# One plan for a block's mixers: chunk ends among the levels, tiles taken out a row later, masks in the exponent

## The chip, the cores and the metric

The kernel runs on one core of a Trainium2 chip. The metric is the device time of one execution in microseconds. The engines are TensorE (PE; PEld for its weight loads), VectorE (DVE), ScalarE (ACT), GpSimd (POOL) and SyncE (SP), which issues most DMAs. Each works through its own queue in program order; semaphores tie the queues together.

## The reference

Two transformer blocks are computed in sequence over 512 tokens of 1024 columns, all in float32. The change touches the mixers of the first block only:

```
proj = einsum('bsd,de->bse', h, w_in)               # 26.5 units of 256 columns, 25 of them in the changed part
o_a = diff attention: softmax(q1 k1) - lam * softmax(q2 k2), times v, 4 heads, 4 query blocks of 128
o_b = hgrn2: gated recurrence S_t = diag(a_t) S_(t-1) + k_t v_t^T, o_t = S_t^T q_t, forward + backward, 4 heads
o_c = gla:   the same recurrence, forward + backward, 4 heads (two at a time here)
merged = g_a * (o_a @ w_up_a) + g_b * (o_b @ w_up_b) + g_c * (o_c @ w_up_c)
x = x + gt_m * (merged @ w_out)
```

The vector `mod` (shift, gain, gate of each part) is `silu(c) @ ada_w + ada_b`; two thirds of it are needed only behind the mixers. The MLP of the first block and the whole second block (windowed attention, a spatial gating unit, two gated FFNs) follow.

## The kernel before

A dense product is made of units: 8 x 128 rows of a weight by 256 columns, 1 MB, loaded by SP into RAW (two buffers, 8 KB a partition), split in four parts into a high half WH (ACT, `split`) and a low half WL (POOL), and multiplied in three passes (HHI x WH, HLO x WH, HHI x WL). A unit gives two tiles of 128 x 512 in PSUM, each of 24 matmuls; a "natural" unit (cv, bv, av) has the tokens on the partitions and 96 matmuls of 256 columns. Each tile is taken out of PSUM (`evict`) by ACT or DVE.

A recurrence r (0 and 1 for gla, two heads each; 2 to 5 for hgrn2, one head each) treats chunks of 128 tokens in seven levels of halves (lv 0 to 6) and one of single tokens (lv 7). A level is `differ` (DVE: Am less a reference column, into DD), `expo` (ACT: exp of each half, in place), `scale` (DVE: KL = k x DD over all columns, then QL for the lower and the upper half, each with a 0/1 vector that switches off one direction), `product` (PE: 4 matmuls of 128 x 128 in float32 for a head) and `collect` (DVE, under a mask, into SCT). DD, QL and KL have two buffers each, by level; the product has PSUM banks 4 and 5 in turns. After the last level come the chunk ends, one after the other: `ends`, `reach` (POOL), `turn` (PE), `state` (PE), `carry` (DVE), `read` (PE). `lag` makes Am out of the cumulated decay with two DVE instructions.

Attention takes a head and a block of 128 queries in four steps: logits for both maps (PE), bias, maximum and scaled maximum (DVE), exponent (ACT), weights (DVE), transposes (PE) and a copy to WT (ACT). The values follow once a head, in one product of 512 columns (`attend_v`), then the head's norm.

The order is set by generators of steps, each step a list of operations that every engine's program walks through alike, skipping what is not its own. `merged` mixes streams by weights. The first merge (from 124 us) mixes `gla` with `projections` (units bz, bq, bv, bg, av, aq, ak and the decays); units cv and cg and the low-rank gate stand ahead of it. The second (from 336 us) mixes `hgrn`, `attention` and `gates`: 12 gate units, whose tiles go through T0 to DRAM (`spill`), and the 16 later units of `ada_w`, which DVE multiplies by eight instructions of 256 columns each. A tile is taken out in the step right behind its last matmul. Behind the second merge the units `up` read all of o_a, o_b, o_c and the spilled gates.

```
    def first_merge(self):
        return merged((self.gla(), WA[0]), (self.projections(), WA[1]))
    def second_merge(self):
        return merged((self.hgrn(), WB[0]), (self.attention(), WB[1]), (self.gates(), WB[2]))
```

Of the kernel before, what the change touches and what calls it, by code (L numbers as in the profile page):

```python
# [7 lines left out]
ACT = mybir.ActivationFunctionType  # L8
# [3 lines left out]
T = 512  # L12
EPS = 1e-6
LAM_INIT = 0.2
KB = 1024
# [5 lines left out]
WA = (77, 110)  # L21
WB = (142, 72, 130)


# [33 lines left out]
def unit_order():  # L58
# [10 lines left out]
    cols("w_in", "cv", full, [(3072, 256)])  # L69
    cols("w_in", "cg", full, [(3328, 256)])  # L70
    for p in range(2):
        c = []
        for h in (2 * p, 2 * p + 1):
            c += [(1792 + 64 * h, 64), (2048 + 64 * h, 64)]
        cols("w_in", "bz", full, c)
    cols("w_in", "bq", full, [(1536, 256)])
    cols("w_in", "bv", full, [(2304, 256)])
    cols("w_in", "bg", full, [(2560, 256)])
    for i in range(2):
        cols("w_in", "av", full, [(1024 + 256 * i, 256)])  # L80
    for i in range(2):
        cols("w_in", "aq", full, [(256 * i, 256)])
        cols("w_in", "ak", full, [(512 + 256 * i, 256)])
    a = 8
    for j in range(4):
        for g in range(3):
            cols("w_in", "gate", full, [(3616 + 1024 * g + 256 * j, 256)])
            for _ in range(2 if g == 0 else 1):
                cols("ada_w", "ada", full, [(256 * a, 256)])
                a += 1  # L90
# [115 lines left out]

def merged(*streams):

    live = [[iter(s), n, 0] for s, n in streams]
    out = []  # L210
    while live:
        x = min(live, key=lambda q: q[2] / q[1])
        step = next(x[0], None)
        if step is None:
            live.remove(x)
        else:
            out += step
            x[2] += 1
    return out


class Plan:


    def __init__(self):
# [16 lines left out]
        self.first = self.first_merge()  # L242
        self.second = self.second_merge()
# [29 lines left out]
    def place(self):  # L273

        at, four, six, seven = self.at, [0, 1, 2, 3], list(range(6)), list(range(7))
        for tag, n, m in (("cqk", 0, 2), ("lr", 0, 1), ("cv", 0, 2), ("cg", 0, 2), ("bz", 0, 2), ("bz", 1, 2), ("bq", 0, 2), ("bv", 0, 2),
                          ("bg", 0, 2), ("av", 0, 2), ("av", 1, 2), ("aq", 0, 2), ("ak", 0, 2), ("aq", 1, 2), ("ak", 1, 2)):
            self.take(four, *[(at[tag, n], j) for j in range(m)])
        self.take([3], *[(at["gate", n], m) for n in range(12) for m in range(2)])
# [40 lines left out]
    def rows(self, tag, n):  # L320

        i = self.at[tag, n]
        nx = self.after(i)
        part = {(0, 2): 0, (0, 4): 1, (0, 6): 2, (1, 0): 3}
        for m in range(2):
            for k in (0, 2, 4, 6):
                yield [("gemm", i, m, k)] + ([("split", nx, part[m, k])] if (m, k) in part else [])
            yield [("evict", i, tag, n, m)]

    def rows_nat(self, tag, n):  # L330
        i = self.at[tag, n]
        nx = self.after(i)
        for g in range(2):
            for h in range(2):
                yield [("nat", i, g, h)] + ([("split", nx, 2 * h), ("split", nx, 2 * h + 1)] if g == 0 else [])
            yield [("evict", i, tag, n, g)]

    def projections(self):
        for p in range(2):
            yield from self.rows("bz", p)  # L340
            yield []
        for p in range(2):
            yield from (self.rows_nat("bv", 0) if p else self.rows("bq", 0))
            yield []
            for n in range(7):
                yield [("decay", p, n)]
        yield from self.rows("bg", 0)
        yield []
        for i in range(2):
            yield from self.rows_nat("av", i)  # L350
            yield []
        for i in range(2):
            for tag in ("aq", "ak"):
                yield from self.rows(tag, i)
                yield []

    def recur(self, r):
        yield [("lag", r)]
        yield [("differ", r, 0)]
        yield [("expo", r, 0), ("differ", r, 1)]  # L360
        yield [("scale", r, 0), ("expo", r, 1)]
        for lv in range(8):
            yield [("product", r, lv)]
            yield [("scale", r, lv + 1)] * (lv < 6) + [("differ", r, lv + 2)] * (lv < 5)
            yield [("collect", r, lv)] + [("expo", r, lv + 2)] * (lv < 5)
        yield [("ends", r)]
        yield [("reach", r)]
        yield [("turn", r)]
        yield [("state", r)]
        yield [("carry", r)]  # L370
        yield [("read", r)]

    def gla(self):
        for n in range(3):
            yield [("gate_c", n)]
        for P in range(2):
            yield from self.recur(P)
            for n in range(3):
                yield [("norm", "c", P, n)]

    def hgrn(self):
        for u in range(2):
            for h in range(2):
                yield from self.recur(2 + 2 * u + h)
            for n in range(3):
                yield [("norm", "b", u, n)]

    def attention(self):
        for h in range(4):
            for qb in range(4):  # L390
                for n in range(4):
                    yield [("attn", h, qb, n)]
            yield [("attn_v", h)]
            for n in range(3):
                yield [("norm", "a", h, n)]

    def gates(self):
        a, left = 8, []
        for j in range(4):
            for g in range(3):  # L400
                n = 3 * j + g
                i = self.at["gate", n]
                nx = self.after(i)
                rows = [[("gemm", i, m, k)] if k < 8 else [("evict", i, "gate", n, m)] for m in range(2) for k in (0, 2, 4, 6, 8)]
                yield left + rows[0]
                yield rows[1]
                at = 2
                for _ in range(2 if g == 0 else 1):
                    for s in range(3):
                        yield [("ada", a, s)] + rows[at]  # L410
                        at += 1
                    a += 1
                part = 0
                for row in rows[at:]:
                    if row[0][0] == "gemm":
                        row = row + [("split", nx, part)]
                        part += 1
                    yield row
                left = [("split", nx, p) for p in range(part, 4)]
        yield left  # L420

    def first_merge(self):
        return merged((self.gla(), WA[0]), (self.projections(), WA[1]))

    def second_merge(self):
        return merged((self.hgrn(), WB[0]), (self.attention(), WB[1]), (self.gates(), WB[2]))


def build(nc, wts, xt, vec, mixc, masks, distw, wst, bsr, out, spill):
# [57 lines left out]
    KBt = place("KBt", q0 + 36 * KB, [4, T])  # L487
    GB = place("GB", q0 + 44 * KB, [2, T])
    QB = place("QB", q0 + 48 * KB, [4, T])
# [11 lines left out]
    DD = [place(f"DD{i}", f + 2 * KB * i, [T]) for i in range(2)]; f += 4 * KB  # L501
    QL = [place(f"QL{i}", f + 2 * KB * i, [T]) for i in range(2)]; f += 4 * KB
    KL = [place(f"KL{i}", f + 2 * KB * i, [T]) for i in range(2)]; f += 4 * KB
# [7 lines left out]
    SB = [place(f"SB{i}", q0 + 64 * KB + 2 * KB * i, [T]) for i in range(2)]  # L511
    WT = place("WT", q0 + 68 * KB, [4, T])
# [28 lines left out]

    sgn = {"c": ("sgnc", "fc", "bc", 1.0 / 16.0), "b": ("sgnh", "fh", "bh", 1.0)}

    def scan(r):

        if r < 2:
            return (QKC[:, r, 0, :], QKC[:, r, 1, :], PC[:, r, :], [(0, 64, 128 * r, 0), (64, 64, 128 * r + 64, 64)], VC, "c",
                    ("qc", 0), ("qc", 1), ("decay_c", r), ("vc", 1))
        h = r - 2
        return (QB[:, h, :], KBt[:, h, :], ZB[:, h, :], [(0, 128, 64 * h, 64 * (h % 2))], VB, "b",  # L550
                ("qb", h // 2), ("kb", h), ("decay_b", h), ("vb", 1))

# [5 lines left out]
    def branch(kind, n):  # L558
        if kind == "a":
            return 0, 2, 128, ones, SC[:, 3:4], None, (OA[:, n, 0, :], OA[:, n, 1, :]), T0[1][:, :], SS[:, :]  # L560
# [45 lines left out]

    FOLD = (0, 3, 6)
    FOLD = (0, 3, 6)
# [3 lines left out]
    def sync_program(q):  # L612
# [20 lines left out]
        for step in P.first + P.second:  # L633
# [9 lines left out]
            if step[0] == "split" and step[2] == 3 or step[0] == "ada" and step[2] == 1:  # L643
                i = step[1] if step[0] == "split" else U["ada", step[1]]
                while done < min(i + 2, len(units) - 1):
                    done += 1
                    load(done)
# [35 lines left out]
    def tensor_program(q):  # L683
# [208 lines left out]
        tiles_nat(U["cv", 0], hk("mix"))  # L892
# [1811 lines left out]
```

## Time and profile before

| what | value |
| --- | --- |
| median of 3 runs | 2562.35 us (2560.0 to 2563.56) |
| the profiled execution's own time | 2563.16 us |
| its span, first to last instruction | 2561.3 us |
| mean granted TensorE clock | 0.962 of full speed |
| PE, DVE, ACT, POOL busy | 92%, 48%, 38%, 41% of the span |
| instructions | 30127 |

The profile's own execution is 0.8 us above the median. Busy shares are of the whole span. PEclk is the clock that TensorE was granted, in parts of full speed; matmuls are pipelined and their ends are modelled, so PE may read as busy while it runs at the lower clock. In a row of groups the idle time and what ended it stand behind the bar.

### The profile page before, as it was taken

The page shows a single profiled execution, that of the slowest core. Times are in us where ns is not written, and L with a number is a line of the kernel's source. Part 1 is how long each engine was busy: PE and PEld are TensorE (multiplying, and loading weights), DVE is VectorE, ACT ScalarE, POOL GpSimd, SP SyncE. Part 2 cuts the span into 40 slices and gives each one's busy share as a digit, 9 for nine tenths or more (in the row PEclk, how much of TensorE's full clock was granted, in tenths as well). Part 3 has the DMA queues.
Part 4 walks back from the last instruction along what each step waited for, and adds up shares of the span by engine and source line. Part 5 has one row for each costly group of instructions (what it writes and reads, how often), then busy time and mean ns, then how long its engine had stood idle before and what let it go on. Part 6 is the DMA issues. An engine that isn't in the chain of part 4 may idle for free. (4 is left out here: it accounts for less than half of the span.)

```text
span 2561.3 us, 30127 instructions
## 1 busy us (share of the span) xinstructions
PE 2346.7 (92%) x12110; PEld 1962.7 (77%) x12110; DVE 1228.5 (48%) x1968; ACT 965.8 (38%) x1801; POOL 1046.0 (41%) x806
## 2 busy tenths in 40 slices
PE   5868987887799999999889999999999999999997
PEld 4656865665488888887678888888988888888887
DVE  4165376788455222146557624445143444743354
ACT  2345233344445233244436322235332224522233
POOL 2333322223154444453134444445444444454443
PEclk9877998889899999999999999999999999999999
DMA  5321133332342222232011222222222222232221
GB/s 214 105 66 50 50 111 103 119 120 100 115 172 83 99 99 83 98 109 71 28 50 67 99 99 98 100 83 99 86 80 99 82 95 72 81 116 84 102 94 66
DMA packets 42508, 239.87 MB, mean 94 GB/s; under 512 B 4992, under 2 KB 7040, under 8 KB 17152
## 3 DMA queue, kind: packets, MB, share of 16 engines
q1 hardware_dynamic: 39312, 231.23, 25.5%
q10 hardware_dynamic: 3056, 6.70, 0.9%
q8 instruction: 96, 1.57, 0.2%
q14 instruction: 44, 0.36, 0.0%
HBM read 226.38 MB, written 8.39 MB: 92 GB/s over the span
## 5 line engine op out<-in xcount | busy, mean ns | idle before, releaser
L2427 POOL TENSOR_TENSOR WL<-RAW,WH 128x512 fp32r<-128x512 f32 (+1 forms) x724 | 949.8, 1342 | 1220.9 <-ACT WH L1212 1209.2
L695 PE MATMUL PS<-HHI,WH 128*128 128x512 f32 (+1 forms) x1688 | 667.0, 395 | 31.4 <-DVE HLO L1759 8.9
L695 PE MATMUL PS<-HHI,WL 128*128 128x512 f32 (+1 forms) x1688 | 646.7, 383 | 0.0
L695 PE MATMUL PS<-HLO,WH 128*128 128x512 f32 (+1 forms) x1688 | 646.4, 383 | 0.0
L1212 ACT ACTIVATE WH<-RAW 128x512 fp32r<-128x512 f32 (+1 forms) x724 | 395.9, 612 | 386.1 <-PE PS L695 362.0
L695 PEld LDWEIGHTS PS<-HHI,WH 128*128 128x128 f32 x1688 | 324.2, 192 | 114.9 <-issue 23.5
L695 PEld LDWEIGHTS PS<-HHI,WL 128*128 128x128 f32 x1688 | 323.7, 192 | 61.8
L695 PEld LDWEIGHTS PS<-HLO,WH 128*128 128x128 f32 x1688 | 324.9, 192 | 57.2 <-issue 1.9
L695 PE MATMUL PS<-UF,WH 128*128 128x512 f32 (+1 forms) x832 | 223.9, 357 | 0.0
L1753 DVE TENSOR_TENSOR T<-PS,R 128x512 f32<-128x512 f32 x112 | 76.9, 689 | 215.4 <-PE PS L695 204.8
L695 PEld LDWEIGHTS PS<-UF,WH 128*128 128x128 f32 x832 | 148.3, 189 | 22.7
L695 PE MATMUL PS<-WH,HHI 128*128 128x256 f32 x544 | 160.1, 294 | 4.4 <-DVE HLO L1759 2.4
L695 PE MATMUL PS<-UP,WH 128*128 128x512 f32 x512 | 157.7, 389 | 0.0
L695 PE MATMUL PS<-WH,HLO 128*128 128x256 f32 x544 | 156.8, 288 | 0.0
L695 PE MATMUL PS<-WL,HHI 128*128 128x256 f32 x544 | 156.6, 288 | 0.0
L1753 DVE TENSOR_TENSOR Y<-PS,Y 128x512 f32<-128x512 f32 x96 | 66.1, 690 | 176.3 <-PE PS L695 176.3
L695 PE MATMUL PS<-UF,WL 128*128 128x512 f32 (+1 forms) x416 | 148.3, 356 | 0.0
L695 PEld LDWEIGHTS PS<-WH,HHI 128*128 128x128 f32 x544 | 107.2, 197 | 10.1 <-POOL WL L2427 3.8
L695 PEld LDWEIGHTS PS<-UP,WH 128*128 128x128 f32 x512 | 96.1, 188 | 20.0
L695 PEld LDWEIGHTS PS<-WH,HLO 128*128 128x128 f32 x544 | 107.5, 198 | 0.3 <-issue 0.2
L695 PEld LDWEIGHTS PS<-WL,HHI 128*128 128x128 f32 x544 | 107.2, 197 | 0.0
L1695 ACT ACTIVATE TG<-TG 128x512 f32<-128x512 f32 x44 | 27.8, 632 | 207.0 <-DVE TG L1759 207.0
(328 smaller groups left out, 3329.4 us busy)
## 6 DMA issues: line engine op xcount, KB each, us to landing
RAW<-in_wts SPq DMA_DIRECT2D x192, 1024.0 KB, 4.8
spill<-T SPq DMA_DIRECT2D x24, 256.0 KB, 5.5
RAW<-in_wts SPq DMA_DIRECT2D x8, 768.0 KB, 4.3
GT<-spill SPq DMA_DIRECT2D x20, 256.0 KB, 5.0
FW<-in_wts SPq DMA_DIRECT2D x4, 1024.0 KB, 15.5
X<-in_xt SPq DMA_DIRECT2D x1, 2048.0 KB, 16.7
out_x<-X SPq DMA_DIRECT2D x16, 128.0 KB, 1.7
X<-in_xt SPq DMA_DIRECT2D x2, 768.0 KB, 9.9
```

The costliest lines, as they stand in the source:

```text
L695: return e.matmul(o_, l, r, start=start, stop=stop)
L1212: e.activation(WH[s][:, cs], RAW[i % 2][:, cs], ACT.Copy).then_inc(*up("w_hi", ("w_hi", i, p)))
L1695: e.activation(G, G, ACT.Gelu_apprx_tanh).then_inc(*up("a_ev", ("gelu", name, j)))
L1753: return e.tensor_tensor(o_, a, b, f)
L2427: return e.tensor_tensor(o_, a, b, f)
```

## The change

- Both merges become one row of steps. `placed` gives each stream a first row and a gap: the 25 dense units have 8 rows each (a row is two k-slices of a tile, 6 matmuls); all recurrences run in one stream from row 9, a step every 1.1 rows; attention from row 75, a step every 1.7; the decays of hgrn2 from rows 19 and 30. cv and cg join the row.
- The levels of all six recurrences form one sequence, so that the first levels of r + 1 are prepared beside the last of r; the chunk ends of r stand among its own levels 1 to 5, `read` and the norm in those of r + 1.
- A tile is taken out at the second row of the tile behind it.
- The 0/1 vector moves into the exponent, as a bias of 0 or -1e30. DD is 2 x 512 wide: `expo` has two more ACT instructions, with that bias, for the q part; `scale` is one DVE instruction of 1024 columns over q and k, which stand side by side (QKC, QKB). QL and KL are gone.
- `lag` is two ACT copies for hgrn2 and four for gla.
- The product has one bank for hgrn2 (4). Dense tiles have four banks up to unit 8, then 3 and 5.
- Attention's values are made by blocks of 128 queries, one block later; WT holds one block. WT and SB no longer share memory with GT.
- The 16 later ada units are cut as 4 row blocks by 512 columns and stand one in each of the dense units 8 to 23: DVE works 8 instructions of 512 columns for a pair of them, and PE folds a pair at once.

```diff
-WA = (77, 110)
-WB = (142, 72, 130)
+DENSE = [("cv", 0), ("bz", 0), ("bz", 1), ("cg", 0), ("bq", 0), ("bv", 0), ("av", 0), ("aq", 0), ("ak", 0), ("av", 1), ("aq", 1), ("ak", 1),
+         ("bg", 0)] + [("gate", n) for n in range(12)]
+GATE_C, DECAY, RECUR, ATTEND = (1, 2), ((19, 1.5), (30, 1.5)), (9, 1.1), (75, 1.7)
...
+def placed(*streams):
+    at = [(start + gap * i, s, i, step) for s, (steps, (start, gap)) in enumerate(streams) for i, step in enumerate(steps)]
+    return [x for *_, step in sorted(at, key=lambda p: p[:3]) for x in step]
...
+            for m in range(2):
+                for row in range(4):
+                    r = 4 * m + row
+                    step = [("nat", i, m, row // 2)] * (row % 2 == 0) if natural else [("gemm", i, m, 2 * row)]
+                    yield step + beside[r] + (late if row == 1 else [])
+                late = [("evict", i, tag, n, m)]
...
+        for r in range(6):
+            for k in range(8):
+                g = 7 * r + k
+                one, two, three = [("product", r, k)], [], [("collect", r, k)]
+                if k < 7 and g + 1 < len(LEVELS):
+                    two.append(("scale", *LEVELS[g + 1]))
+                if k < 7 and g + 2 < len(LEVELS):
+                    two.append(("differ", *LEVELS[g + 2]))
+                    three.append(("expo", *LEVELS[g + 2]))
...
         def expo(r, lv):
-            e.activation(D[:, :, 0:m], D[:, :, 0:m], ACT.Exp, scale=-s).then_inc(*up("a_mix", ("expo_lo", r, lv)))
-            e.activation(D[:, :, m:2 * m], D[:, :, m:2 * m], ACT.Exp, scale=s).then_inc(*up("a_mix", ("expo", r, lv)))
+            e.activation(Q[:, :, 0:m], K[:, :, 0:m], ACT.Exp, scale=-s, bias=SC[:, b[0]:b[0] + 1])
+            e.activation(Q[:, :, m:2 * m], K[:, :, m:2 * m], ACT.Exp, scale=s, bias=SC[:, b[1]:b[1] + 1]).then_inc(*up("a_mix", ("expo_q", r, lv)))
+            q.wait_ge(*at(("expo_q", r, lv)))
+            e.activation(K[:, :, 0:m], K[:, :, 0:m], ACT.Exp, scale=-s)
+            e.activation(K[:, :, m:2 * m], K[:, :, m:2 * m], ACT.Exp, scale=s).then_inc(*up("a_mix", ("expo", r, lv)))
...
         def scale(r, lv):
-            tt(Ko, Ki, D, MUL)
-            stt(Qo[:, :, 0:m], Qi[:, :, 0:m], v(bs), D[:, :, 0:m], MUL, MUL)
-            stt(Qo[:, :, m:2 * m], Qi[:, :, m:2 * m], v(fs), D[:, :, m:2 * m], MUL, MUL).then_inc(*up("d_mix", ("scaled", r, lv)))
+            D = level(r, lv)[:, :, :]
+            tt(D, both, D, MUL).then_inc(*up("d_mix", ("scaled", r, lv)))
...
+    def product_bank(r, n):
+        return 4 + (n if r < 2 else 0)
```

Two places of the queues show it. On DVE, in an hgrn2 recurrence beside attention; KL, QL, DD and SCT are the recurrence's, SB and SC attention's, SQ and MOD the ada units'. Before, two levels:

```order
L1753 TENSOR_TENSOR KL_106<-KBt,DD_102 128x512
L1759 SCALAR_TENSOR_TENSOR QL_104<-QB,V,DD_102 128x32x8 x2
L1753 TENSOR_TENSOR DD_101<-Am,ZB 128x512
L2083 RECIPROCAL SC<-SC 128x2
L1756 TENSOR_SCALAR SB_116<-SB_116,SC 128x512
L1759 SCALAR_TENSOR_TENSOR SB_115<-SB_115,SC,SB_116 128x512
L2017 COPY_PREDICATED SCT_107<-MASK,PS 128x512
L1753 TENSOR_TENSOR KL_105<-KBt,DD_101 128x512
L1759 SCALAR_TENSOR_TENSOR QL_103<-QB,V,DD_101 128x64x4 x2
L1753 TENSOR_TENSOR DD_102<-Am,ZB 128x512
```

After, two levels:

```order
L1765 TENSOR_TENSOR DD_101<-QKB,DD_101 128x1024
L1765 TENSOR_TENSOR DD_100<-Am,ZB 128x512
L1765 TENSOR_TENSOR MOD<-PS,V 128x4
L2015 COPY_PREDICATED SCT_102<-MASK,PS 128x512
L1768 TENSOR_SCALAR SQ<-RAW_64,CC 128x512
L1771 SCALAR_TENSOR_TENSOR SQ<-RAW_64,CC,SQ 128x512
L1765 TENSOR_TENSOR DD_100<-QKB,DD_100 128x1024
L1765 TENSOR_TENSOR DD_101<-Am,ZB 128x512
```

Three instructions of a level's scaling have become one; the ada work comes in pairs of 512 columns.

On ACT, in the same part of the program; WH is a split, T a gate tile taken out, SB the two exponents of an attention block, WT its weights. Before:

```order
L1438 ACTIVATE DD_102<-DD_102 128x32x8
L1533 ACTIVATE T_74<-PS 128x512
L1497 ACTIVATE SB_115,SC<-SB_115,SC 128x512
L1497 ACTIVATE SB_116,SC<-SB_116,SC 128x512
L1212 ACTIVATE WH_66<-RAW_63 128x512
L1437 ACTIVATE DD_101<-DD_101 128x64x4
L1438 ACTIVATE DD_101<-DD_101 128x64x4
```

After:

```order
L1508 ACTIVATE SB_110,SC<-SB_110,SC 128x512
L1508 ACTIVATE SB_111,SC<-SB_111,SC 128x512
L1441 ACTIVATE DD_101<-DD_101,SC 128x32x8
L1442 ACTIVATE DD_101<-DD_101,SC 128x32x8
L1444 ACTIVATE DD_101<-DD_101 128x32x8
L1445 ACTIVATE DD_101<-DD_101 128x32x8
L1541 ACTIVATE T_74<-PS 128x512
L1514 ACTIVATE WT<-PS 128x512
```

A level has four exponents instead of two, and they still stand behind attention's two.

## Rows read from the trace of the kernel before

**Rows 1.** The page: busy time, and the span in 40 slices.
```profile
PE 2346.7 (92%) x12110; PEld 1962.7 (77%) x12110; DVE 1228.5 (48%) x1968; ACT 965.8 (38%) x1801; POOL 1046.0 (41%) x806
...
PE   5868987887799999999889999999999999999997
PEclk9877998889899999999999999999999999999999
```

**Rows 2.** Busy time of each engine by stretch, whose columns the second line names.
```profile
core 0: us, PE busy (x) PEld busy (x) DVE busy (x) ACT busy (x) POOL busy (x), PEclk, DMA share, GB/s
92.00:124.00 32.00, 32.00 (x175) 28.34 (x175) 3.85 (x15) 9.71 (x16) 12.16 (x11) 0.91 0.27 99
124.00:336.00 212.00, 176.82 (x1012) 144.78 (x1010) 110.58 (x176) 97.19 (x149) 78.80 (x54) 0.87 0.17 58
336.00:650.00 314.00, 251.33 (x1116) 187.10 (x1115) 246.36 (x461) 118.75 (x251) 83.39 (x59) 0.89 0.33 112
650.00:692.00 42.00, 23.06 (x83) 13.75 (x83) 13.88 (x36) 22.13 (x39) 8.87 (x8) 0.80 0.12 39
```

**Rows 3.** The same view, of a stretch inside the first merge and one behind it.
```profile
250.00:325.00 75.00, 75.00 (x481) 62.50 (x480) 28.57 (x57) 22.76 (x45) 24.00 (x19) 1.00 0.20 71
875.00:900.00 25.00, 25.00 (x112) 20.71 (x111) 4.27 (x6) 7.81 (x15) 11.51 (x10) 1.00 0.24 85
```

**Rows 4.** Groups of instructions, 80 to 692 us: a level of a recurrence.
```profile
L1753 DVE TENSOR_TENSOR KL<-KBt,DD 128x512 f32<-128x512 f32 x28 | 25.7, 918 | 0.3 <-ACT DD L1438 0.2
L1759 DVE SCALAR_TENSOR_TENSOR QL<-QB,V,DD 128x256 f32<-128x256 f32 x56 | 36.7, 696 | 0.0
L1753 DVE TENSOR_TENSOR DD<-Am,ZB 128x512 f32<-128x512 f32 x28 | 23.3, 833 | 0.0
L1437 ACT ACTIVATE DD<-DD 128x256 f32<-128x256 f32 x42 | 17.6, 419 | 72.2 <-DVE DD L1753 72.0
L2017 DVE COPY_PREDICATED SCT<-MASK,PS 128x512 f32<-128x512 uint8 x56 | 39.2, 727 | 17.5 <-PE PS L695 17.5
L1753 DVE TENSOR_TENSOR ZB<-ZB,G 128x1024 f32<-128x1024 f32 x4 | 4.9, 1220 | 1.2 <-ACT G L1431 1.1
```

**Rows 5.** One line's instructions, least, median and longest ns, 336 to 689 us.
```profile
L1759 DVE SCALAR_TENSOR_TENSOR SQ<-RAW,CC,SQ x112: 466/485/1502, 340.2 to 637.7; 128x256 f32<-128x256 f32 x112
L1759 DVE SCALAR_TENSOR_TENSOR QL<-QB,V,DD x56: 471/478/1518, 342.2 to 641.3; 128x256 f32<-128x256 f32 x56
```

**Rows 6.** Groups as in Rows 4: what else moves.
```profile
L1759 DVE SCALAR_TENSOR_TENSOR SQ<-RAW,CC,SQ 128x256 f32<-128x256 f32 x112 | 59.7, 533 | 3.6
L1759 DVE SCALAR_TENSOR_TENSOR G<-G,LB,G 128x512 f32<-128x512 f32 x4 | 2.8, 747 | 2.4 <-ACT G L1428 2.4
L1756 DVE TENSOR_SCALAR Am<-ZB,V 128x512 f32<-128x512 f32 x4 | 3.2, 793 | 0.0
L1451 ACT ACTIVATE KH<-Am,SC 128x128 f32<-128x128 f32 x24 | 9.9, 483 | 13.0 <-DVE SC L1756 13.0
```

**Rows 7.** Instructions in order of time, from four places of the mixers.
```profile
270.21 1.71 PE L695 MATMUL PS<-QL,KL 64*128 64x128 f32 x16
...
304.14 0.60 PE L916 MATMUL PS<-V,KH 128*128 128x128 f32 x4
...
474.81 0.72 ACT L1497 ACTIVATE SB<-SB,SC 128x512 f32<-128x512 f32 x1 [6.61 <-DVE SC L1756]
...
484.85 1.13 PE L695 MATMUL PS<-QK 64*128 64x512 f32 x4
```

**Rows 8.** Waits, 336 to 689 us: sum, times, longest.
```profile
ACT SB L1497 <- DVE SC L1756: 69.6, 25, 10.6
ACT DD L1437 <- DVE DD L1753: 45.2, 18, 6.6
```

**Rows 9.** Instructions in order of time: the first and the last of the mixers.
```profile
92.64 0.58 PE L695 MATMUL PS<-WH,HHI 128*128 128x256 f32 x1
...
689.79 0.74 PE L695 MATMUL PS<-OA,WH 128*128 128x512 f32 x2 [3.53 <-POOL OA L2427]
```

More of the change, by code:

```diff
@@ L241, in __init__ @@
         self.place()
-        self.first = self.first_merge()
-        self.second = self.second_merge()
+        self.steps = placed((self.projections(), (0, 1)), (self.gate_c(), GATE_C), (self.decays(0), DECAY[0]), (self.decays(1), DECAY[1]),
+                            (self.recurrences(), RECUR), (self.attention(), ATTEND))
     def slot(self, i):
@@ L357, in recur @@
[L357 to L371, printed above, removed]
@@ L373, in gla @@
-    def gla(self):
+    def projections(self):
+        late = []
+        for tag, n in DENSE:
+            i = self.at[tag, n]
+            nx = self.after(i)
+            natural = tag in NATURAL
+            ada = i + 1 if nx > i + 1 else None
+            beside = [[] for _ in range(8)]
+            for p in range(4):
+                beside[2 * (p // 2) if natural else 1 + p].append(("split", nx, p))
+            if ada:
+                a = [u for u in range(8, 24) if self.at["ada", u] == ada][0] - 8
+                for part, row in ((0, 2), (1, 4)):
+                    beside[row].append(("ada", a // 2, a % 2, part))
+                if a % 2:
+                    beside[6].append(("fold", a // 2))
+                    beside[7].append(("mod", a // 2))
+            for m in range(2):
[4 more added lines that the diff above has]
+                late = [("evict", i, tag, n, m)]
+        yield late
@@ L374, in gla, with gate_c, decays @@
+    def gate_c(self):
         for n in range(3):
             yield [("gate_c", n)]
[L376 to L386, printed above, removed]
+    def decays(self, p):
+        for n in range(7):
+            yield [("decay", p, n)]
@@ new lines, in recurrences @@
+    def recurrences(self):
+        box = {0: ("c", 0), 1: ("c", 1), 3: ("b", 0), 5: ("b", 1)}
+        yield [("lag", 0)]
+        yield [("differ", 0, 0)]
+        yield [("expo", 0, 0), ("differ", 0, 1)]
+        yield [("scale", 0, 0), ("expo", 0, 1)]
+        for r in range(6):
[7 more added lines that the diff above has]
+                    three.append(("expo", *LEVELS[g + 2]))
+                if k == 0 and r:
+                    two.insert(0, ("read", r - 1))
+                elif k == 1:
+                    one.append(("ends", r))
+                elif k == 2:
+                    two.append(("reach_k", r))
+                    three.append(("turn", r))
+                elif k == 3:
+                    two.append(("state", r))
+                elif k == 4:
+                    one.append(("carry", r))
+                    one.append(("eq", r))
+                elif k == 5 and r < 5:
+                    one.append(("lag", r + 1))
+                if k == 5:
+                    two.append(("reach_q", r))
+                if k > 3 and r - 1 in box:
+                    three.append(("norm", *box[r - 1], k - 4))
+                yield one
+                yield two
+                yield three
+        yield [("read", 5)]
+        for n in range(4):
+            yield [("norm", *box[5], n)]
@@ L388, in attention @@
     def attention(self):
+        late = [[], [], [], []]
         for h in range(4):
             for qb in range(4):
[L391 to L420, printed above, removed]
@@ L429, in build @@
+                yield (late[2] if qb == 0 else []) + [("attn", h, qb, 3)]
+            late = [[("norm", "a", h, n)] for n in range(4)]
+        yield [("attn", 3, 3, 4)]
+        yield from late
 def build(nc, wts, xt, vec, mixc, masks, distw, wst, bsr, out, spill):
@@ L631, in sync_program @@
         done = 9
-        for step in P.first + P.second:
+        for step in P.steps:
             if step[0] == "evict" and step[2] == "gate":
```

389 lines of the change are left out of this document (175 added, 214 removed).

## The prediction

> **What bounds the kernel now.** I first read the page: PE is busy 92% of the span, and both its slices and its granted clock sag from about the second to the eleventh of 40 [rows 1]. So the time is PE's, except in the mixers. The busy time by stretch says why they are slow [rows 2]: in the first merge (124 to 336 us) PE is busy 176.8 of 212 us at a granted clock of 0.87; in the second up to 650 us it is busy 251.3 of 314 at 0.89, while DVE, at 246.4 of 314 (78%), is nearly as full; from 650 to 692 nothing is full, which is a tail of attention and its norm. A busy PE at 0.87 is a mixture of its two levels: 2.4 GHz, and 1.2 GHz after idling. The views of other stretches show what is possible: 250 to 325 us, a recurrence beside projections without attention, has PE busy all of 75 us at clock 1.00 [rows 3].
>
> Next I price PE's work in the mixers at full clock. 112 matmuls of 512 columns fill 25.00 us behind the mixers, 0.223 us each [rows 3], so a unit of 48 is 10.7 us (a natural unit has the same columns). Sixteen product records took 1.71 us, that is 0.214 us for a float32 matmul of 128 columns and 0.855 us for a head's four [rows 7].
> - Dense: 25 x 10.7 = 267.5.
> - Products: 64 x 0.855 = 54.7 (2 x 8 levels of two heads, 4 x 8 of one).
> - Attention: 16 blocks of logits at 1.13 [rows 7] = 18.1, transposes at 0.60 (as the transposes of KH in [rows 7]) = 9.6, values at 0.855 = 13.7; sum 41.4.
> - Reads 64 x 0.214 = 13.7, eight norm means x 0.855 = 6.8, turns 6 x 0.60 = 3.6, states 32 x 0.107 = 3.4, folds of the ada sums about 10; sum 37.5.
>
> Total 401 us. From the first matmul of cv at 92.6 us to the one that waited for the last output of attention, 689.8 us [rows 9], it takes 597 us. So 196 us are idle time or low clock. What is waited for in the second merge is order: ACT stands 69.6 us before attention's exponents for DVE's maxima, with the recurrence's exponents queued behind, and 45.2 us for `differ` [rows 8]; one such stand is 6.61 us [rows 7].
>
> **The change, part by part.**
> 1. *Scaling in one instruction.* A level's DVE work was KL 0.918, QL 2 x 0.696, `differ` 0.833 and `collect` 0.727, or 3.87 us [rows 4]. The new one multiplies two SBUF operands over 1024 columns; the nearest row is ZB<-ZB,G at 1.22 us [rows 4]. KL and QL's means are above their medians, of which the trace shows QL's: 0.478, with a longest of 1.518 us [rows 5]; some instructions stand 1.0 us for something. The mean delay of a QL is 0.22 us. If it comes per instruction, the new one takes 1.22 + 0.22 = 1.44 us and a level saves 2.31 - 1.44 = 0.87 us, 37 us in 42 levels. If delays go with the time that instructions take, the new one takes about 1.22 x 0.696 / 0.478 = 1.78 us and it saves 22 us. I take 37: long instructions were not seen to be delayed more often (the four of 1024 columns had 1.22 as their mean).
>    The Trainium skill (SBUF — State Buffer, "SBUF: two separate sides") calls this an exclusive lock: a DVE instruction with two SBUF inputs and a GpSimd one that reads SBUF block each other for a whole instruction. The longest rows fit it; by that rule the delay is per meeting, as in the first case, and the sum is the same 37.
> 2. *ada.* 112 instructions at 0.533 (and 16 of the first kind, about the same) are 67 us [rows 6]; now 64 of 512 columns, nearest row G<-G,LB,G at 0.747 [rows 6], are 48 us. DVE saves 19 us. They are also spread over 16 units, from unit 8 on, instead of 12.
> 3. *lag.* Two DVE instructions at about 0.79 [rows 6] six times, 9 us, leave DVE; 16 ACT copies of 32 or 64 partitions are bounded by 0.2 and 0.7 us each, 3 to 11 us.
> 4. *Exponents.* 84 more on ACT. Plain ones take 0.419 [rows 4]; ones with a scale and a bias from SBUF take 0.483 at half the columns [rows 6], so up to 0.55. That is 35 to 46 us on ACT. A level's chain grows by about 1.1 us, which two DD buffers and a row's distance cover. If the cover is gone (ACT late), `scale` is late and then the product.
>    After this DVE has 371 (the sums of [rows 2]) - 37 - 19 - 9 = 306 us of work in the mixers, ACT 238 (its sum in [rows 2]) + 40 + 7 = 285, both well under PE's 401.
> 5. *Order.* This is the large part. 201 rows replace two merges. cv and cg, which ran with PE full, cover the gate's and the first level's preparation; the chunk ends, which were a chain of six engine changes per recurrence, lie beside levels; tiles are taken out later, so ACT and DVE don't stand for a tile's last matmul; and attention ends at row 191 of 201, so the tail from 650 us goes, of which PE's work at most half fills 42 us.
>    I cut the row at 75, where attention starts. Rows 0 to 74 hold 9.4 units and both gla recurrences: 142 us of PE. ACT is the likelier limit near rows 19 to 40, where both decays stand with their table loads. I take PE's share there as 0.79, between the 0.67 of all the mixers before and the 1.00 of [rows 3]: 180 us. Rows 75 to 200 hold 15.6 units, nearly four hgrn2 recurrences, attention and ada: 259 us of PE against some 225 of DVE. The old fullest engine reached 0.78 there; with two engines at 259 and 225, but shorter stands, I take 0.85: 305 us.
> 6. *SP, POOL, memory.* The same bytes are loaded; ada and dense units alternate and each has a unit's time (some 18 us) to land. POOL keeps its work. SP's spills and reloads keep their order. Cost nothing, because a unit takes longer than its load; were a load late, `split` on ACT would show it.
>
> Sum: the `up` units start at 92.6 + 180 + 305 = 578 us instead of 689.8, 112 us earlier. Nothing behind is changed (from 692 us PE is bound by itself), so the execution's own 2563.2 becomes 2451; against the median, 0.8 lower, **2450 us**.
>
> **Rivals.**
> - *The rows run in lockstep* (chance 0.18). Every engine walks the same rows with a row or less of slack, and load per row is uneven: a row with attention's maxima has some 3.1 us of DVE (two of about 0.69 + 0.69 + 0.15 each), then ACT's exponents in the same row, with the recurrence's behind. If a row costs its fullest engine, rows 75 to 200 take about 3.05 us, 384, and the first 75 take 2.4, 180. The sum is 657 us to `up`, gain 33: 2530, between 2505 and 2550. For it: the stands in [rows 8] have this form and are not removed. Against it: DVE has 0.87 us less a level, and the rows spread the rest.
> - *PE becomes the bound nearly everywhere* (0.15). As in 250 to 325 us; at a share of 0.94, 401 becomes 427, gain 170 less some 10 for the decays: 2403, between 2385 and 2420. For it: DVE and ACT both have a quarter of their time free. Against it: rows of unequal load.
> - *Slower, through the one bank of hgrn2's products* (0.08). The product of a level stands at PE's head until DVE has collected the one before; what DVE has in between can be a whole attention block, 3.1 us of maxima and 1.9 of weights, so 5 us. If PE, with the dense matmuls queued behind, stood that long at each of 32 products, 160 us would be lost: 2611. It decides the sign from 112 / 32 = 3.5 us per product. Against it: in the queue, `collect` stands a row ahead of the next product, and a row is over 2 us.
> - *No change* (0.04): the saved time returns wholly as such stands; 2563.
>
> **How the numbers follow.** The forecast itself has 0.55 and runs from 2420 to 2490 (0.79 and 0.85 could each be off by 0.07, and ACT's exponents by 11 us). The range 2390 to 2545 holds it, the upper two thirds of the PE-bound case and most of lockstep, and leaves out some 0.18. A measurement of this kernel can tell 0.2%, 5 us, from no change. Faster: 0.55 + 0.18 + 0.15 = 0.88, of which I give 0.02 to slower and 0.01 to the same, since a restructuring of this size can meet a wait that I have not seen; so 0.85, 0.05, 0.10.
>
> **What would show it.** In the changed profile: `up` starting near 578 us; DVE's 1024-column multiply at 1.2 to 1.5 us, 42 times; DVE near 306 and ACT near 285 us busy before `up`; granted clock over 0.93 in the mixers; PE busy some 85% from unit av on. Wrong, if PE's waits for SCT grow past 3 us each (the bank), if ACT's wait for the maxima stays near 70 us with a row at 3 us (lockstep), if the multiply takes 1.8 us, or if the part behind `up` changed by more than a few us.

## The result, and the profile after

The changed kernel takes 2465.5 us (median; 2465.0 to 2467.2) against 2562.7: a ratio of 0.9624, 95% interval 0.9607 to 0.9640, or 97 us less where 112 were forecast. The forecast of 2450 was 15 us low.

The page of the changed kernel, its busy times and slices, as in [rows 1]:

```profile
PE 2316.2 (94%) x12206; PEld 1958.2 (79%) x12206; DVE 1204.2 (49%) x1806; ACT 1013.2 (41%) x1902; POOL 1059.0 (43%) x806
...
PE   4889988899999999998889999999999999999997
PEclk9999989899999999999999999999999999999999
```

The sag from the second to the eleventh slice is gone but for a little; the granted clock has two 8s left, in the sixth and the eighth slice. The first and the last matmul of the mixers, as in [rows 9]:

```profile
90.71 0.58 PE L691 MATMUL PS<-WH,HHI 128*128 128x256 f32 x1
...
584.23 0.62 PE L691 MATMUL PS<-OA,WH 128*128 128x512 f32 x2
```

They run from 90.7 to 584.2 us, 493.5 us instead of 597.2. The forecast had 485. (The 1.9 us of earlier start lie ahead of the changed part; I did not follow them.) The span of this profile is 2465.5 us, and its own time, 2467.2, is 1.7 above the median. What lies behind is not the same as before: 2465.5 - 584.2 = 1881.3 us against 2561.3 - 689.8 = 1871.5. So the end of the mixers moved by 105.6 us, and 9.8 were given back later.

The same view as [rows 2], of the changed kernel. The third line of times starts with attention's first logits, at 262.8 us; the last is the end of the `up` units:

```profile
core 0: us, PE busy (x) PEld busy (x) DVE busy (x) ACT busy (x) POOL busy (x), PEclk, DMA share, GB/s
90.00:124.00 34.00, 33.48 (x200) 29.08 (x200) 18.96 (x40) 23.09 (x44) 17.90 (x14) 0.94 0.26 93
124.00:262.00 138.00, 125.82 (x811) 103.90 (x810) 98.70 (x139) 94.47 (x158) 61.67 (x38) 0.96 0.20 69
262.00:584.00 322.00, 286.52 (x1449) 228.12 (x1448) 232.81 (x346) 175.24 (x350) 115.65 (x79) 0.94 0.33 120
584.00:629.00 45.00, 43.91 (x194) 36.05 (x192) 24.99 (x38) 26.15 (x47) 18.87 (x15) 1.00 0.73 268
629.00:639.00 10.00, 5.36 (x17) 4.33 (x18) 7.43 (x12) 4.27 (x8) 2.95 (x4) 0.66 0.30 107
```

PE is busy 286.5 of 322 us beside attention, at a clock of 0.94 instead of 0.89, and DVE 232.8, or 72%, instead of 78%. Over the whole of the mixers PE was busy 483.2 of 600 us before (the sum of [rows 2]) and is busy 445.8 of 494 now. So of the 106 us between the two stretches 69 are idle time that is gone, and 37 are shorter busy time for nearly the same matmuls, at a higher clock.

The 9.8 us that were given back come in three parts. In the last line PE is busy 5.4 of 10 us at a clock of 0.66: from the first `up` matmul to the first one of the output product the changed kernel takes 49.4 us, and three kernels of experiments 1 and 10, which leave one line out, take 43.6; that is 5.8 us. Another 2.0 us are a matter of counting: in the kernel before, nine `up` matmuls ran at 683.6 us, ahead of the one at 689.8 from which I count. The last 2 us are small differences in clock and stands, such as the low clock in these two stretches, the changed kernel's first, then the same place before (an estimate of its worth: at most 0.07 x 50 = 3.5 us):

```profile
684.00:734.00 50.00, 47.41 (x280) 42.66 (x279) 25.33 (x38) 22.23 (x41) 24.41 (x18) 0.93 0.30 104
```

```profile
789.80:839.80 50.00, 50.00 (x291) 44.46 (x291) 22.96 (x36) 25.21 (x46) 22.13 (x16) 1.00 0.24 85
```

The groups that answer to [rows 4] and [rows 6], columns as there:

```profile
L1771 DVE SCALAR_TENSOR_TENSOR SQ<-RAW,CC,SQ 128x512 f32<-128x512 f32 x56 | 61.3, 1095 | 2.8 <-DMA RAW<-in_wts 1.6
L1765 DVE TENSOR_TENSOR DD<-QKB,DD 128x1024 f32<-128x1024 f32 x28 | 42.2, 1508 | 4.9 <-ACT DD L1445 4.8
...
L1765 DVE TENSOR_TENSOR DD<-Am,ZB 128x512 f32<-128x512 f32 x28 | 28.0, 1002 | 17.3 <-PE PS L691 17.3
...
L1441 ACT ACTIVATE DD<-DD,SC 128x256 f32<-128x256 f32 x42 | 21.5, 511 | 49.7 <-DVE DD L1765 49.7
...
L1765 DVE TENSOR_TENSOR DD<-QKC,DD 128x1024 f32<-128x1024 f32 x14 | 17.7, 1266 | 10.5 <-ACT DD L1445 10.4
...
L2431 POOL TENSOR_TENSOR KH<-KH,QKB 128x512 f32<-128x512 f32 x8 | 13.7, 1712 | 0.3 <-ACT KH L1467 0.3
```

The multiply of 1024 columns has a mean of (42.2 + 17.7) / 42 = 1.43 us; 1.44 were forecast. But the ada instruction of 512 columns takes 1.095 us instead of 0.747, `differ` 1.00 instead of 0.83, and POOL's product KH 1.71, where the unhindered one takes 1.29. One line's instructions (least, median, longest), as in [rows 5]:

```profile
L1771 DVE SCALAR_TENSOR_TENSOR SQ<-RAW,CC,SQ x53: 731/752/1783, 260.9 to 561.7; 128x512 f32<-128x512 f32 x53
```

The median, 0.752 us, is close to the 0.747 of the row that I had taken; the longest is 1.03 us more, which is less than one POOL instruction (the least WL takes 1.26). The mean holds a delay of 0.34 us for each, but they do not share it evenly. 22 of the 56 began while a POOL instruction ran; these 22, and no other, are longer, by 0.90 us each. In the kernel before it was 6 of 112, by 0.94 us each. So one meeting costs what it did, and there are more of them. POOL is busy 36% of the stretch beside attention (115.65 of 322 us) where it was busy 27% (83.39 of 314); that alone does not make seven times the share of meetings, and no run shows what else does. A multiply that starts inside a POOL instruction, and one that meets none:

```profile
310.19 1.71 POOL L2431 TENSOR_TENSOR WL<-RAW,WH 128x512 fp32r<-128x512 f32 x1
310.70 2.28 DVE L1765 TENSOR_TENSOR DD<-QKB,DD 128x1024 f32<-128x1024 f32 x1
...
316.92 1.22 DVE L1765 TENSOR_TENSOR DD<-QKB,DD 128x1024 f32<-128x1024 f32 x1
```

The waits of ACT beside attention (270 to 584 us), as in [rows 8], and those of PE from 90 to 584 us:

```profile
ACT SB L1508 <- DVE SC L1768: 59.6, 29, 6.0
...
ACT DD L1441 <- DVE DD L1765: 24.3, 10, 5.1
```

```profile
PE PS L691 <- DVE SCT L2015: 25.3, 12, 8.0
PE PS L951 <- ACT SS L1496: 14.0, 3, 6.5
PE PS L909 <- POOL KH L2431: 2.7, 2, 2.0
```

ACT still stands 59.6 us for attention's maxima. PE's own stands are few: 25.3 us for `collect` (SCT), 14.0 us for the logarithm of attention's norm (SS). The same view of the kernel before, 92 to 690 us, shows what has gone:

```profile
PE PS L695 <- DVE SQ L1759: 26.5, 8, 6.4
PE PS L695 <- DVE QL L1759: 21.5, 9, 8.8
PE PS L695 <- DVE SCT L2017: 13.8, 2, 6.9
PE PS L957 <- DVE SB L1759: 12.0, 6, 7.5
```

There PE stood 26.5 us for ada's sums (SQ), now 2.6, and 21.5 us for the scaled operands (QL), now 0.5 (DD). In all PE is not busy in 48 of these 494 us. The other 45 us above the 401 of the price list are only in part work at the lower clock: a mean of 0.94 over 494 us is worth at most 30 us, so the list itself is short by some 15.

### The profile page after: what moved, and what is told of

The parts are those of the page before. It is cut to its first block and busy times, and to the rows that moved or that the text cites. A ratio compares the mean times of both kernels' runs of the same rounds, so it can differ in the third digit from the quotient of the medians.

```text
span 2465.5 us, 30245 instructions
## 1 busy us (share of the span) xinstructions
PE 2316.2 (94%) x12206; PEld 1958.2 (79%) x12206; DVE 1204.2 (49%) x1806; ACT 1013.2 (41%) x1902; POOL 1059.0 (43%) x806
## 5 line engine op out<-in xcount | busy, mean ns | idle before, releaser
L1771 DVE SCALAR_TENSOR_TENSOR X<-PS,MOD,X 128x512 f32<-128x512 f32 (+1 forms) x56 | 37.0, 672 | 142.8 <-PE PS L691 142.8
L691 PEld LDWEIGHTS PS<-WH,HLO 128*128 128x128 f32 x544 | 105.6, 194 | 0.3 <-issue 0.2
## 6 DMA issues: line engine op xcount, KB each, us to landing
X<-in_xt SPq DMA_DIRECT2D x2, 768.0 KB, 10.5
```

Of the source, the lines that this page charges most:

```text
L691: return e.matmul(o_, l, r, start=start, stop=stop)
L1771: return e.scalar_tensor_tensor(out=o_, in0=a, scalar=s, in1=b, op0=f1, op1=f2)
```

## The experiments

All are edits of the changed kernel, except the one in the old order. The kernel before, run beside each group, stayed between 2563 and 2565 us, so a few us between two kernels mean something only where intervals part.

**1. The banks of the `up` tiles (e1_ring).** In `place`, the diff had one more reset of the bank counter ahead of the ring of seven:

```diff
             self.take(four if d < 9 else [3, 5], (at[tag, n], 0), (at[tag, n], 1))
-        self.turn = 0
         self.take(seven, *[(at["up", j], m, g) for j in range(4) for m in range(2) for g in range(3)])
```

> The changed kernel, whose up tiles again start their seven PSUM banks where the dense tiles left off (one line less), so that the first tiles of the output product don't fall on the banks of the last up tiles. If the 5.7 us stand of PE at 633.6 us and the low clock around it come from this ring: 7 to 10 us less, near 2457 us, and no PE wait over 1 us there. If they come from the gates' reload, which now starts 1.6 us behind the first up matmul instead of beside the last wait: no change, 2465 us within 2.

Measured: 2455.0 us, ratio 0.9584 (0.9561 to 0.9606), 10.5 us less by the medians; the intervals of the two kernels only just part. The stand in the changed kernel, in order of time, and the place in this run (whose profiled execution was the longest of its four, by 8 us; only what lies behind the mixers is read here):

```profile
633.64 1.22 PE L691 MATMUL PS<-ME,WH 128*128 128x512 f32 x2 [5.73 <-DVE GT L1765]
```

```profile
634.56 0.73 PE L690 MATMUL PS<-ME,WH 128*128 128x512 f32 x2 [0.17 <-POOL WL L2430]
```

With the reset, the last `up` tiles lie in banks 0, 1 and 2, and the first tiles of the output product need bank 0. It is emptied only when DVE has reached the last gate sums. Without it the counter goes on, the last tiles lie in 4, 5 and 6, and the output product starts on banks that are long free. The first theory holds. The traces price it better than the medians do: behind the first `up` matmul the changed kernel has 1881.3 us, and the three kernels without the reset have 1874.3 (this one), 1873.9 (e8_three) and 1873.3 (e12_best). So the reset costs 7 to 8 us: the stand of 5.7 us, and some 1.5 us for the first matmuls behind it, of which six take 2.7 us (633.64 to 636.36) where six at full clock take 1.36. What the medians show beyond that is not parted from the spread of the runs.

**2. The masks back on DVE (e2_masks_on_dve).**

```diff
-            e.activation(Q[:, :, 0:m], K[:, :, 0:m], ACT.Exp, scale=-s, bias=SC[:, b[0]:b[0] + 1])
-            e.activation(Q[:, :, m:2 * m], K[:, :, m:2 * m], ACT.Exp, scale=s, bias=SC[:, b[1]:b[1] + 1])
...
-            tt(D, both, D, MUL)
+            stt(Q[:, :, 0:m], Qi[:, :, 0:m], v(bs), K[:, :, 0:m], MUL, MUL)
+            stt(Q[:, :, m:2 * m], Qi[:, :, m:2 * m], v(fs), K[:, :, m:2 * m], MUL, MUL)
+            tt(K, both[:, 1, :], K, MUL)
```

> The changed kernel with the masks back on DVE (two exponents a level instead of four, one multiply of 512 columns and two masked ones of 256 instead of one of 1024), in the new order. If DVE's queue is what the rows wait for most: DVE gains some 35 us of work, ACT loses some 43, and the time rises by 15 to 30 us, to 2480 to 2495. If ACT's longer chain of exponents costs as much as DVE saves: 2465 within 5. If ACT is what the rows wait for: 10 us less or better.

Measured: 2463.1 us, ratio 0.9607 (0.9589 to 0.9625): no difference that can be told. The busy times up to `up` (PE, PEld, DVE, ACT, POOL, as in the window views), first of this run, then of the changed kernel:

```profile
90.00:578.00 488.00, 440.62 (x2468) 356.23 (x2467) 369.18 (x608) 257.60 (x470) 188.76 (x130) 0.96 0.29 106
```

```profile
90.00:584.00 494.00, 445.82 (x2456) 361.10 (x2456) 350.47 (x524) 292.80 (x550) 195.22 (x129) 0.94 0.29 104
```

DVE has 19 us more work, ACT 35 less, and the time stays within what these runs can tell, some 6 us. DVE's 32 us of extra scaling came out as 19, since its other instructions met POOL less (16 of 56 ada sums, not 22):

```profile
L1768 DVE SCALAR_TENSOR_TENSOR SQ<-RAW,CC,SQ 128x512 f32<-128x512 f32 x56 | 55.8, 997 | 2.7 <-DMA RAW<-in_wts 1.5
...
L1768 DVE SCALAR_TENSOR_TENSOR DD<-QKB,V,DD 128x256 f32<-128x256 f32 x56 | 39.1, 739 | 1.5 <-ACT DD L1442 1.2
...
L1762 DVE TENSOR_TENSOR DD<-Am,ZB 128x512 f32<-128x512 f32 x28 | 23.5, 838 | 8.1 <-PE PS L691 8.0
```

(0.997 and 0.838 for the ada sums and `differ`, instead of 1.095 and 1.002.) The second case of the expectation holds. In the new order no gain of the masks in the exponent can be told; the run doesn't part a small gain on DVE from a small loss through ACT.

**3. The masks in the exponent alone, in the old order (e7_masks_old_order).** The kernel before with `expo` and `scale` of the change, DD two wide and q beside k; the merges untouched.

```diff
-            e.activation(D[:, :, 0:m], D[:, :, 0:m], ACT.Exp, scale=-s).then_inc(*up("a_mix", ("expo_lo", r, lv)))
-            e.activation(D[:, :, m:2 * m], D[:, :, m:2 * m], ACT.Exp, scale=s).then_inc(*up("a_mix", ("expo", r, lv)))
...
+            e.activation(Q[:, :, 0:m], K[:, :, 0:m], ACT.Exp, scale=-s, bias=SC[:, b[0]:b[0] + 1])
...
+            e.activation(K[:, :, 0:m], K[:, :, 0:m], ACT.Exp, scale=-s)
...
-            tt(Ko, Ki, D, MUL)
-            stt(Qo[:, :, 0:m], Qi[:, :, 0:m], v(bs), D[:, :, 0:m], MUL, MUL)
...
+            tt(D, both, D, MUL).then_inc(*up("d_mix", ("scaled", r, lv)))
```

> The kernel before, its two merges and all its order kept, with the masks in the exponent and one multiply of 1024 columns (q and k side by side). If the forecast's step 1 held: DVE was the fullest engine there (246 of 314 us) and loses some 37 us, so 15 to 30 us less than 2563. If a level's longer chain through ACT takes back what DVE saves: within 5 us of 2563. If ACT's stands grow: slower by 10.

Measured: 2556.3 us, ratio 0.9967 (0.9954 to 0.9980), 9 us less. In its stretch from 336 to 650 us (as [rows 2]) DVE fell from 246.4 to 237.9 us and ACT rose from 118.8 to 149.3:

```profile
336.00:650.00 314.00, 247.90 (x1144) 184.32 (x1141) 237.94 (x428) 149.34 (x322) 90.02 (x61) 0.92 0.34 117
```

So where DVE was nearly full the part gave 9 us, between the first two cases of the expectation; beside the new order no such gain can be told.

**4. A tile taken out at once (e3_evict_at_once).**

```diff
-                    yield step + beside[r] + (late if row == 1 else [])
-                late = [("evict", i, tag, n, m)]
+                    yield step + beside[r] + ([("evict", i, tag, n, m)] if row == 3 else [])
```

> The changed kernel with each tile taken out in the row of its last matmuls instead of two rows later. If the late row matters, ACT and DVE stand for PE at 50 tiles, a matmul row each or up to 1 us, and the time rises by 10 to 30 us. If the order alone has given the gain, it stays within 3 us of 2465.

Measured: 2478.3 us, ratio 0.9665 (0.9646 to 0.9683). The late row is worth 13 us. The first case of the expectation holds. ACT's wait for PE ahead of a gate tile, here from 90 to 582 us, then in the changed kernel from 270 to 584 us:

```profile
ACT T L1540 <- PE PS L690: 35.1, 15, 6.0
```

```profile
ACT T L1541 <- PE PS L691: 4.8, 2, 2.7
```

**5. The chunk ends behind the levels (e9_ends_behind).** `recurrences` is written as before: four steps of preparation, eight levels, seven steps of ends, the norm, and nothing of the next recurrence beside it. The stream has 226 steps instead of 153, so its gap had to become 0.84 rows to end in time; the run changes both.

```diff
-GATE_C, DECAY, RECUR, ATTEND = (1, 2), ((19, 1.5), (30, 1.5)), (9, 1.1), (75, 1.7)
+GATE_C, DECAY, RECUR, ATTEND = (1, 2), ((19, 1.5), (30, 1.5)), (9, 0.84), (75, 1.7)
...
-                if k == 0 and r:
-                    two.insert(0, ("read", r - 1))
-                elif k == 1:
-                    one.append(("ends", r))
...
+                yield [("product", r, k)]
+                yield [("scale", r, k + 1)] * (k < 6) + [("differ", r, k + 2)] * (k < 5)
+                yield [("collect", r, k)] + [("expo", r, k + 2)] * (k < 5)
+            yield [("ends", r)]
+            yield [("reach_k", r)]
```

> The changed kernel with each recurrence by itself again in its stream: four steps of preparation, eight levels, then the six steps of the chunk ends and the norm, none beside another's levels; 226 steps of 0.84 rows, so that the stream ends at row 199. If the levels in one sequence with the chunk ends among them carry a good part of the order's gain: 20 to 50 us more, 2485 to 2515. If any stream that is spread over the 201 rows does as well: within 6 us of 2465.

Measured: 2515.2 us, ratio 0.9812 (0.9796 to 0.9829), 50 us more. PE's waits in this run:

```profile
PE PS L673 <- DVE DD L1747: 29.6, 6, 10.1
PE PS L673 <- DVE SCT L1997: 27.9, 10, 5.2
```

PE now stands 29.6 us for the scaled operands (DD), a wait of 0.5 us in the changed kernel. All six of these waits stand before the first product of a recurrence; the two longest, of recurrences 1 and 2:

```profile
208.87 3.09 PE L673 MATMUL PS<-DD 64*128 64x128 f32 x16 [10.10 <-DVE DD L1747]
```

```profile
295.35 2.08 PE L673 MATMUL PS<-DD 128*128 128x128 f32 x8 [8.85 <-DVE DD L1747]
```

So they are not the price of the faster pace within a recurrence, where a level has 2.5 rows instead of 3.3. They are the price of its start: `lag`, `differ`, `expo` and `scale` follow each other, 0.84 rows apart, with no product of the recurrence before beside them. The first theory holds: half of the gain is this sequence. Of the 50 us 29.6 are these six stands; how the rest divides between the overlap of the chunk ends and the pace, this run does not part.

**6. Attention's exponents a step later (e4_exponents_later).** ACT takes the exponents one step behind DVE's maxima; five steps of 1.36 rows a block.

```diff
-GATE_C, DECAY, RECUR, ATTEND = (1, 2), ((19, 1.5), (30, 1.5)), (9, 1.1), (75, 1.7)
+GATE_C, DECAY, RECUR, ATTEND = (1, 2), ((19, 1.5), (30, 1.5)), (9, 1.1), (75, 1.36)
...
+                yield [("attn", h, qb, 5)]
...
-            if n == 1:
+            if n == 5:
```

> The changed kernel with attention in five steps of 1.36 rows instead of four of 1.7: the exponents stand one step behind the maxima on ACT's queue. If the rows run in lockstep there (ACT stood 65 us for the maxima, with the recurrence's exponents behind): 10 to 25 us less. If PE's order hides these stands already: within 3 us of 2465.

Measured: 2460.4 us, ratio 0.9599 (0.9580 to 0.9619); the interval overlaps that of the changed kernel. ACT's waits (90 to 582 us):

```profile
ACT DD L1442 <- DVE DD L1766: 60.4, 25, 4.9
...
ACT SB L1509 <- DVE SC L1769: 24.5, 19, 4.9
```

The wait for the maxima fell from 64.1 us (of the changed kernel from 90 to 584 us) to 24.5 us, and the wait for `differ` rose from 49.7 to 60.4. At best 5 us came of 40: ACT's stands are hidden. This was the ground of the lockstep rival.

**7. The norm's mean in bank 0 (e5_mean_bank0).**

```diff
-            return 2, 1, 128, ones, SC[:, 3:4], None, (OA[:, n, 0, :], OA[:, n, 1, :]), T0[1][:, :], SS[:, :]
+            return 2, 0, 128, ones, SC[:, 3:4], None, (OA[:, n, 0, :], OA[:, n, 1, :]), T0[1][:, :], SS[:, :]
```

> The changed kernel with the mean of attention's norm in PSUM bank 0 instead of bank 1, where the transposes of the next head's first block wait for its logarithm. If those three stands (14.0 us on PE) are on the path: 8 to 14 us less. If the rows behind make up for them: within 3 us of 2465.

Measured: 2459.7 us, ratio 0.9591 (0.9578 to 0.9604), 6 us less. The stand for SS is gone from PE's waits, but one for the norm's result (T) has come:

```profile
PE PS L691 <- DVE SCT L2015: 26.3, 13, 8.0
PE PS L691 <- DVE T L1771: 9.4, 3, 4.9
```

A part of the stands was on the path: 14.0 us are gone, 9.4 have come, and the time is 6 us less, just under the range expected.

**8. Short ada sums (e6_ada_short).** Each ada instruction takes 8 columns instead of 512; the later parts of mod are thereby left out.

```diff
-                w_ = r[:, 512 * kk:512 * kk + 512]
+                w_, ac = r[:, 512 * kk:512 * kk + 8], SQ[:, 0:8]
```

> The changed kernel with the later ada sums cut to 8 of 512 columns on DVE (the later parts of mod are left out; loads, folds and waits stay). DVE loses some 55 of its 351 us. If DVE's load is what PE waits for in the rows with attention: 15 to 35 us less. If only the order of stands between engines counts, as the masks' run suggests (32 us more of scaling on DVE, time unchanged): less than 6 us.

Measured: 2451.7 us, ratio 0.9561 (0.9547 to 0.9576), 14 us less, between the two cases. DVE's busy time from 90 to 584 us fell from 350.5 to 322.1, and that window now also holds 14 us of `up`; up to the first `up` matmul at 569.6 us it is 315.0, so 35 us less. DVE's load is worth something, some 14 us of 35, but it is not what the rows run at.

**9. Attention from row 100 (e10_attention_late)** and **a wider spread (e11_even).** Only the two pairs of numbers are changed: `ATTEND` to (100, 1.7); and `RECUR` to (9, 1.2), `ATTEND` to (75, 1.8).

```diff
-GATE_C, DECAY, RECUR, ATTEND = (1, 2), ((19, 1.5), (30, 1.5)), (9, 1.1), (75, 1.7)
+GATE_C, DECAY, RECUR, ATTEND = (1, 2), ((19, 1.5), (30, 1.5)), (9, 1.1), (100, 1.7)
```

> The changed kernel with attention starting at row 100 instead of 75 at the same pace, so that it ends 14 rows behind the last gate tile. If the tail of attention without dense work beside it was a large part of what was lost before (42 us at 650 to 692 us): two blocks of about 10 us and a norm lie bare, 20 to 40 us more, 2485 to 2505. If less load at rows 75 to 100 gives it back: within 8 us of 2465.

```diff
-GATE_C, DECAY, RECUR, ATTEND = (1, 2), ((19, 1.5), (30, 1.5)), (9, 1.1), (75, 1.7)
+GATE_C, DECAY, RECUR, ATTEND = (1, 2), ((19, 1.5), (30, 1.5)), (9, 1.2), (75, 1.8)
```

> The changed kernel with the recurrences a step every 1.2 rows and attention every 1.8, so that both end near row 191 and 197 and the last 24 rows don't hold gates alone. If uneven load of the rows costs what is lost in the mixers: 5 to 15 us less. If the loss is in stands between engines whatever the load: within 3 us of 2465.

Measured: 2458.0 us, ratio 0.9590 (0.9574 to 0.9605), and 2453.9 us, ratio 0.9571 (0.9555 to 0.9588). In the first the bare tail is there, and it costs something:

```profile
555.00:570.00 15.00, 7.34 (x32) 4.80 (x31) 4.51 (x10) 5.19 (x9) 0.00 (x0) 0.70 0.08 32
```

PE is busy 7.3 of 15 us there, at a clock of 0.70. The rows before more than pay for it: from 313 to 540 us PE is busy 209.7 of 227 us, where it is 198.1 in the changed kernel. So the second case of the expectation holds, less load in the rows from 75 on gives the tail back, and the net is 7 us better. e11_even holds as expected: 12 us less from an even load. In it PE's wait for SS has shrunk to 2.6 us; that the norm's steps have more room there is my reading:

```profile
PE PS L691 <- DVE SCT L2015: 33.9, 10, 7.4
...
PE PS L951 <- ACT SS L1496: 2.6, 3, 1.3
```

**10. Three at once.** e8_three has the ring, bank 0 and the later exponents.

> The changed kernel with the up ring, the norm's mean in bank 0 and attention's exponents a step later, all three. If their gains add up (10 + 10 + 5): near 2440 us. If they hide each other in the mixers, only the ring's 10 us and a little more remain: 2450 to 2455.

Measured: 2453.3 us, ratio 0.9558 (0.9543 to 0.9572): the second case, little more than the ring alone: single gains do not add up. e12_best has the ring, bank 0 and the wider spread, with attention from row 84.

The row numbers of e12_best, beside the reset left out and bank 0 as above:

```diff
-GATE_C, DECAY, RECUR, ATTEND = (1, 2), ((19, 1.5), (30, 1.5)), (9, 1.1), (75, 1.7)
+GATE_C, DECAY, RECUR, ATTEND = (1, 2), ((19, 1.5), (30, 1.5)), (9, 1.2), (84, 1.7)
```

> The changed kernel with the ring of the up tiles as before, the norm's mean in bank 0, a recurrence step every 1.2 rows, and attention from row 84 every 1.7, so that both last until rows 191 and 201. If the gains of the single runs (10 for the ring, 6 for the bank, 12 for the spread) add up: 2436 to 2442 us. If the bank and the spread hide each other: 2444 to 2450. If all three share one cause: no better than 2453.

Measured: 2447.1 us, ratio 0.9542 (0.9529 to 0.9555): the second case again, and the fastest kernel of the study, 18 us under the changed one. PE still waits for SCT there, and now for attention's weights (SB):

```profile
PE PS L690 <- DVE SCT L2014: 21.5, 10, 6.1
PE PS L950 <- DVE SB L1770: 10.2, 4, 4.0
```

## Why the prediction was right, and where it was off

- **What bounds it.** PE in the mixers at 401 us of work, the rest idle or slow: held, though the list of 401 is short by some 15 us. The mixers took 493.5 us where 485 were forecast. Up to attention it was 172 us (forecast 180), beside attention 321 (forecast 305), that is PE shares of 0.83 and 0.81 instead of 0.79 and 0.85. These two shares were chosen between rows and not worked out, and their errors, 8 us one way and 16 the other, cancel in part: that the sum came within 9 us of 485 is partly luck.
- **Step 1, scaling.** The instruction was sized right (1.43 for 1.44 us), by the first of the two rules, a delay per instruction that meets one: 22 of 56 ada sums are longer, by 0.90 us each. The rule of the Trainium skill (SBUF — State Buffer, "SBUF: two separate sides") fits what the trace then showed of both engines: only ada sums that start inside a POOL instruction are longer, and none by more than one POOL instruction. But I applied the delay to the new instruction only. More of the others met POOL too, and ada saved nothing, so DVE's work fell by some 24 us (3.9 + 370.8 to 350.5), not by 65. PE did not wait for it, so the forecast of the time was not hurt. In time the step was worth 9 us in the old order and nothing that can be told in the new.
- **Step 2, ada.** Mis-sized: 61.3 + 5.3 = 66.6 us instead of 48, no saving. The row it was taken from (G<-G,LB,G, 0.747) had four instructions, and none of them had met POOL.
- **Step 3 and 4, lag and exponents.** ACT came to 292.8 us, forecast 285. Masked exponents took 0.51 us, inside their bounds. The longer chain was covered, as said: PE waited 0.5 us for DD.
- **Step 5, order.** The large part, and it is: the sequence of levels and its pace 50 us, the late row 13. What I named as waited for were ACT's stands, and they are still there (69.6 to 59.6 us for the maxima). What went were PE's own, which the prediction did not name: 26.5 us for ada's sums and 21.5 for QL, now 2.6 and 0.5. The tail is a loss where it stands bare (7.3 of 15 us busy in e10_attention_late), but no run gives its share of the gain, since that run also made earlier rows lighter. Some 30 us of the gain (blocks of values, cv and cg inside, ada in 16 units, the tail) were not parted by any run, and since e8_three shows that single gains do not add up, the 30 is a rough figure.
- **Step 6 and the sum, "nothing behind is changed".** This failed. I had read the diff's reset of a bank counter as part of the renumbering and had asked of the part behind only whether its loads and queues moved, not which bank its tiles fall on. It cost 7 to 8 of the 15 us by which the forecast was low; 2 more are the nine `up` matmuls that I had counted as the mixers' work.
- **Rivals.** Lockstep: its stands are in the trace (59.6 us, not far from the 70 that I had named as its sign), but a row beside attention took 321 / 126 = 2.55 us and not 3.05, and taking 40 us of the stands away gave 5 us, which the intervals do not part from nothing. The one bank: 12 waits of 25.3 us in all and 8.0 at the longest; 32 of 3.5 would have been needed. PE nearly full: 493.5 against 427.

## What to carry to other kernels

Price the bounding engine's work at its full rate, and judge a reordering by what share of the stretch that is; instructions saved on an engine with slack, even one that is busy 78%, came to 9 us of 35 and then to none that could be told. When a stage is made to end earlier, look also at what the diff does to the buffers of the stage behind: in which order they come free is as much a part of the order as the queues. Two engines that block each other take back a share of any saving, when more of their instructions meet in the denser stretch. A chain of preparation ahead of a recurrence is cheap only beside the levels of the one before: bare, its six starts cost PE 29.6 us.

## What was not expected of the hardware

The delay that DVE and POOL give each other is one size, and what changes is how often it falls: 6 of 112 ada sums before, by 0.94 us each, and 22 of 56 now, by 0.90 us each. So a 512-column sum of two SBUF operands has a median of 0.752 and a mean of 1.095 us. POOL's product KH went from 1.27 us in the kernel before to a mean of 1.71. And a stand of PE of 5.7 us cost 7 to 8, since six of the matmuls behind it took 2.7 us instead of 1.36; the clock granted from 629 to 639 us had a mean of 0.66.
